# Values' projection of the second block made a filling between the index scores, with the freed fillings spread over the later steps

## What is computed

```python
p = rms_norm(x) @ w_in                # one wide projection, split into the parts below
# branch a: latent attention on the keys that an index picks
score = sum_h iw_h * relu(iq_h @ ik.T)            # 4 index heads, causal
sel   = top_k(score, 64)
y_a   = softmax(q_a @ kv[sel]) @ kv[sel]
# branch b: stick-breaking attention, 8 heads
z = sb_q @ sb_k.T / 8
a = exp(log_sigmoid(z) + sum of log_sigmoid(-z) over later keys)
y_b = a @ sb_v                                     # sb_v: the values
# branch c: gated linear attention on silu(conv(ml_qk)), ml_v, gates ml_i, ml_f, ml_o
y = [y_a * silu(z_a), y_b * silu(z_b), norm(y_c) * silu(z_c)]
x = x + (sum_g sigmoid(merge_g) * (y_g @ w_branch_g)) @ w_out
```

## Time and profile before

| | us |
|---|---|
| median of 3 runs | 1896.74 (1895.46 to 1897.2) |
| the profiled execution's own time | 1890.77 |
| span of its trace | 1889.3 |
| PE busy | 1812.8 (96%) |
| DVE busy | 1086.2 (57%) |
| ACT busy | 871.7 (46%) |

### The profile page before, as it was taken

One profiled execution on the slowest core, in us unless ns is written; L12 is line 12 of the kernel. 1 busy time (PEld: TensorE's weight loads), 2 busy tenths in 40 slices (PEclk: granted clock), 3 DMA queues, 4 the chain that ended last, 5 costly groups with the idle time before them and its releaser, 6 DMA issues.

```text
span 1889.3 us, 30389 instructions
## 1 busy us (share of the span) xinstructions
PE 1812.8 (96%) x12330; PEld 1542.3 (82%) x12330; DVE 1086.2 (57%) x2078; ACT 871.7 (46%) x1519; POOL 320.9 (17%) x148
## 2 busy tenths in 40 slices
PE   6999899999999999999999999998999999899997
PEld 3866576868888888696798999987889999788897
DVE  5356665442110111458867656789647887975676
ACT  4334445333222222345555445547564655655553
POOL 0321222424435444230000000110001001000100
PEclk9999999999999999999999999999999999999999
DMA  9534211254323222447246655563434455343442
GB/s 377 185 134 156 101 57 56 89 189 146 100 90 101 100 99 92 145 134 268 68 134 232 200 193 190 177 203 101 145 112 134 157 189 186 105 134 125 132 146 79
DMA packets 76730, 272.25 MB, mean 144 GB/s; under 512 B 8240, under 2 KB 11568, under 8 KB 76592
## 3 DMA queue, kind: packets, MB, share of 16 engines
q1 hardware_dynamic: 74656, 266.37, 41.6%
q10 hardware_dynamic: 1936, 3.94, 0.6%
HBM read 269.23 MB, written 1.05 MB: 143 GB/s over the span
## 4 chain that ended last, share of the span: by engine, by line
PE 76%; DVE 12%; ACT 7%; issue 2%; DMA 1%; POOL 1%; DVEq 0%; SPq 0%; ACTq 0%
PE bank L1045 22%; PE bank L1047 21%; PE bank L1046 21%; DVE low L1872 3%; ACT high L1465 2%; PE bank L1251 2%; PE bank L1220 2%; PE bank L1129 2%; PE bank L1233 2%; DMA raw<-stream 1%; DVE tmp L2354 1%; PE bank L1346 1%; DVE hx L2226 1%; POOL few L1815 0%; ACT L1691 0%
## 5 line engine op out<-in xcount | busy, mean ns | idle before, releaser
L1045 PE MATMUL bank<-h,high 128*128 128x256 f32 (+1 forms) x2208 | 713.3, 323 | 13.5 <-issue 5.0
L1047 PE MATMUL bank<-h,low 128*128 128x256 f32 (+1 forms) x2208 | 687.3, 311 | 0.0
L1046 PE MATMUL bank<-h,high 128*128 128x256 f32 (+1 forms) x2208 | 687.2, 311 | 0.0
L1465 ACT ACTIVATE high<-raw 128x1024 fp32r<-128x1024 f32 x408 | 426.9, 1053 | 231.8 <-PE bank L1047 226.7
L1045 PEld LDWEIGHTS bank<-h,high 128*128 128x128 f32 x2208 | 416.9, 189 | 85.3 <-issue 44.0
L1872 DVE TENSOR_TENSOR low<-raw,high 128x1024 fp32r<-128x1024 f32 x291 | 364.9, 1260 | 158.8 <-ACT high L1465 158.1
L1047 PEld LDWEIGHTS bank<-h,low 128*128 128x128 f32 x2208 | 416.8, 189 | 26.2
L1046 PEld LDWEIGHTS bank<-h,high 128*128 128x128 f32 x2208 | 417.0, 189 | 22.3
L1806 POOL TENSOR_TENSOR low<-raw,high 128x1024 fp32r<-128x1024 f32 x117 | 284.2, 2435 | 526.9 <-ACT high L1465 526.9
L1916 DVE TENSOR_TENSOR gt<-bank,gt 128x512 f32<-128x512 f32 (+1 forms) x44 | 24.6, 558 | 185.7 <-PE bank L1047 182.9
L1815 POOL TENSOR_TENSOR few<-few,halves 128x2 f32<-128x2 f32 (+2 forms) x19 | 16.4, 861 | 659.8 <-DVE few L1976 659.8
(11 more groups left out here) (314 smaller groups left out, 2767.1 us busy)
## 6 DMA issues: line engine op xcount, KB each, us to landing
raw<-stream SPq DMA_DIRECT2D x504, 512.0 KB, 3.4
xc<-x_in SPq DMA_DIRECT2D x1, 1024.0 KB, 5.5
xc<-ctx_in SPq DMA_DIRECT2D x1, 1024.0 KB, 7.7
cst<-consts ACTq DMA_DIRECT2D x1, 896.0 KB, 8.7
cst<-consts ACTq DMA_DIRECT2D x1, 704.0 KB, 6.9
ukw<-uk ACTq DMA_DIRECT2D x1, 512.0 KB, 6.6
uvw<-uv ACTq DMA_DIRECT2D x1, 512.0 KB, 7.2
out<-xc ACTq DMA_DIRECT2D x1, 512.0 KB, 2.9
```

The source lines that it names most:

```text
L1045: mm(dst, wh, xh, start=start, stop=False)
L1046: mm(dst, wh, xl, start=False, stop=False)
L1047: return mm(dst, wl, xh, start=False, stop=stop)
L1465: do(high[:, i % PAIRS, :], raw[:, slot % SLOTS, :], ACTF.Copy).then_inc(S["hi"], 1)
```

## The change

The values' projection is taken out of its own sweep and becomes the first thing that the fillings give. One piece of filling stands before the first index score, and one after each of the eight, where four stood after every second score. So the eight `SV` pieces stand between the scores, and of the other fillings only one piece is used there instead of sixteen. The fifteen that are freed are used later: 10 instead of 6 between the first `stick` and its `sticklog`, 6 instead of 3 in each of the six rounds of the stick pipeline, 6 instead of 4 before each of the four `gated` steps. The `keep` steps of the first layer go between the scores. `few` now stands ahead of `SV`, which so uses the two filling banks.

```diff
         o.rest()
         o.pool_share = (0, 1)
-        for k, _ in enumerate(o.token("SV", l, 2, 512)):
-            if not l:
-                o.step("keep", k)
 
         def projections():
+            yield from o.token("SV", l, 2, 512)
             for j in range(8):
                 yield from o.linear("CV", l, j)
                 yield from o.linear("Z", l, j)
...
         o.filling.append(projections())
         o.step("few")
+        o.fill(1)
         for t in range(2):
             for hd in range(4):
                 o.step("score", l, t, hd)
-                if hd % 2:
-                    o.fill(4)
+                if not l:
+                    o.step("keep", 4 * t + hd)
+                o.fill(1)
             o.step("scored", l, t)
...
             o.step("stick", l, p)
-            o.fill(6)
+            o.fill(6 if p else 10)
             o.step("sticklog", l, p)
 
-        pipeline([stick, lambda p: o.step("stay", l, p), lambda p: o.step("stuck", l, p)], NH // 2, (4, 3, 3), True)
+        pipeline([stick, lambda p: o.step("stay", l, p), lambda p: o.step("stuck", l, p)], NH // 2, (4, 6, 3), True)
...
                 for part in range(4):
-                    o.fill(4)
+                    o.fill(6)
                     o.step("gated", l, part)
```

## The result

| | us |
|---|---|
| median after, 4 runs | 1926.72 (1925.33 to 1929.66) |
| median before, 4 runs | 1896.1 (1891.92 to 1897.2) |
| ratio after/before | 1.0173, 95% interval 1.0153 to 1.0193 |
| profiled execution after, span | 1929.66, 1928.2 |

The changed kernel is slower, as forecast, but by 30.6 us and not by 11, and the time lies outside the range (1893 to 1918). The two profiled executions are even 38.9 us apart: that of before is faster than all of its timed runs, that of after is the slowest of its four. A second set of runs of both gave 1.0193 (1.0170 to 1.0217), 38.7 us.

A forecast was written before the change was run, and what follows sets the result against it. PE was taken as the bound (busy 1812.8 of 1889.3 us), with DVE nearly full in the `SV` to `MV` stretch. 2.2 - 1.7 + 5.0 = 5.5 us a layer, 11.0 in all, on 1896.74 gave 1907.7 us; range 1893 to 1918.

The forecast's parts named there:

- Part 1: Sweep between the scores: `stay` 0 comes at 27.3 us after the `SV` start, a gain of 0.8 us.
- Part 2: Stick pipeline with six pieces a round: DVE waits for ACT; whole stretch from `SV` to `MV` +2.2 us a layer.
- Part 3: `gated` steps: PE's 1.67 us wait for an `MG` drain goes, -1.7 us a layer.
- Part 4: Layer's end: fifteen fewer pieces behind the last `mean`, so PE waits at the third `BR` tile; +5.0 us a layer.
- The rival of the clock: PE's clock falls behind four stalls a layer, 1.4 us each: 1912 to 1917.5 us; chance 0.20 for 1911 to 1918.
- fillings nearly free: Stretch from `SV` to `MV`: pieces fill PE's idle gaps, giving 6 of 7.6 us, time 1891.3 us; chance 0.12.
- losses of part 2 absent: Stick pipeline: no added DVE waits, the stretch shrinks about 3 us and pays for the end, 1893.0 to 1900.5; chance 0.15.

The follow-up runs named there:

- e1: The changed kernel with its index scores in pairs again, two pieces of `SV` or filling after every second score; ratio to the kernel before 1.0180.
- e6: The kernel before with `SV` as first filling, two pieces after each pair of scores, and the 15 freed pieces in one lump behind `rowsum`; ratio 0.9984.
- e2: The changed kernel with only DVE's order altered: `rows` right behind the last `stuck`, ahead of the `CV` 6 convolution and two splits; ratio to the kernel before 1.0141.
- e8: The kernel before with six pieces instead of four ahead of each `gated`, the eight taken from the layer's end; ratio 1.0007.
- e3: The kernel before with 15 pieces from the layer's end moved ahead, in one lump behind `rowsum`; ratio 1.0033.
- e7: The changed kernel with products without use in front of the waits of `stay` 0 to 2 and the third `BR` tile; ratio to the kernel before 1.0157.
- e12: The changed kernel itself, measured again; ratio to the kernel before 1.0193.
- e11: The kernel of e6 with 10 pieces instead of 6 behind `stick` 0 and a lump of 11; ratio to the kernel before 1.0148.

## Why the prediction was wrong, point by point

- **Part 1, the sweep** (gain 0.8): in the changed kernel `stay` 0 came at 30.0 and not 27.3, and these 2.7 us stayed. The step that failed is the estimate of 0.35 us a score: standing alone it costs 0.63 or 0.84, and e1, with the scores in pairs, is 2 us a layer sooner than a layer of the changed kernel with the same falls of the clock. The gain of 0.5 to 0.7 us in e6 is near the 0.8, but with scores in pairs and six pieces behind `stick` 0, so it does not confirm the working of part 1.
- **Part 2, six pieces a round**: right from `stay` 0 to `stay` 3, 40.1 us forecast and 40.0 measured, and DVE's waits are the forecast ones (PE's are 7.3 us in all and not some 9). DVE, in rounds 1 and 2 of the second layer:

```profile
1649.79 1.23 DVE L1872 TENSOR_TENSOR low<-raw,high 128x1024 fp32r<-128x1024 f32 x1 [1.81 <-ACT high L1465]
1656.15 1.03 DVE L2257 SCALAR_TENSOR_TENSOR tmp<-prob,tmp 128x384 f32<-128x384 f32 x2 [2.43 <-ACT tmp L1691]
1664.19 1.23 DVE L1872 TENSOR_TENSOR low<-raw,high 128x1024 fp32r<-128x1024 f32 x1 [1.81 <-ACT high L1465]
```

  1.8, 2.4 and 1.8 us were named. What failed is the next line of the working: "from `stay` 3 to `MV` stand 44 pieces (15.0 us) ... and about 0.5 of small waits". I walked DVE and ACT step by step up to the last `stay` and only counted PE's pieces behind it. There the stall of 5.0 us stood, with about 2.6 of low clock behind it: 8.1 us missed in this layer, the larger half of the error. e2 shows it: it takes 6.3 of them back, and of the 1.9 that stay 1.0 is what is left of the wait.
- **Part 3, `gated`** (-1.7): e8 gives it in full; in the changed kernel 0.86 us of the wait stayed, since the pieces ahead of it were others.
- **Part 4, the end** (+5.0): right. 9.5 us from `mean` to the third `BR` tile (forecast 9.6), a wait of 3.1 us; e3 and e8 measured it alone. The fall of the clock behind it, 3.0 us by e7 and e12, was put at nothing in the sum (1.8 shows in the difference to before).
- **The rival of the clock** had four stalls of 2.7 to 3.7 us and 1.4 us for each fall, 1917.5 at most. It had the right kind of loss at half its size: a fall behind a long stall costs 2.6 to 3.0 us and not 1.4, and one of the two long stalls was not in the forecast. The falls behind `stay` 0 and 1 came and cost next to nothing (e7); the one behind `stay` 2, which would have cost 1.6, did not come in the profiled execution.
- **The rivals on the fast side** (fillings nearly free, losses of part 2 absent) are refuted by the waits above. The first says that pieces of filling are nearly free, and e6, where only `SV` and the lump have moved, gains, but less than 1 us a layer.

Not settled: how the clock chooses. Stalls of 2.2 to 2.6 us in front of `stay`, and that of 3.1 us at `BR`, were followed by a fall in some layers and not in others of the same program. And the stall of 5.0 us was not refilled in e7, since the bank of the next product is not free there; its share of low clock is taken from the rows, not from a run.

## What to carry to other kernels

A filling is not only PE time: its end puts a drain on ACT and a split on DVE, and where these fall in the order of the dependent steps decides more than how many pieces there are. After such a change follow every engine's order through to the end of the region, also behind the last step that was edited, and look for a drain behind an ACT step that waits for DVE. Where a round has as many pieces as its tiles, a good place holds for all rounds (e6), and so does a bad one (e11); move freed pieces in one lump outside the region rather than spread them. Price a stall of 3 us or more in this kernel at its length plus some 3 us of low clock behind it, and compare two runs only where their falls of the clock stand at the same places: a single fall here hid a gain of 2 us (e1).

## What the runs showed of the hardware

- Behind stalls of 3.1 and 5.0 us the granted clock was 0.50 for 5 to 6 us of matmuls, in seven of eight cases in after and e12. At the layer's end this lost 3.0 us (after against e7, and against the layer of e12 without the fall).
- What a fall costs depends on who sets the pace behind it. Behind stalls of 2.2 to 2.5 us at `stay` 0 and 1 it cost 0.3 us up to `MV` (e7 against after). Behind one of 2.6 us at `stay` 2, with the same loss of 1.7 us by the clock, the next round took 12.3 us instead of 10.7 (the two layers of e12).
- Products without use (3.29 us for 28 matmuls of 128 columns, 0.12 each) put into stalls of 2.2 to 3.2 us, kept the clock at 1.00 behind them (e7).
- Two matmul groups on the two halves of PE's rows, one behind the other, take 0.42 us together; one alone takes 0.41.
